# Layer norm of a four-layer transformer kernel: root applied on ScalarE, offset added by features behind the transposes

## The chip, the cores and the metric

One core of one Trainium2 chip runs the whole program. The metric is the device time of one execution in microseconds. Engines are called TensorE (PE in the profile; PEld is its weight load), VectorE (DVE), ScalarE (ACT), GpSimd (POOL), and SyncE (SP), which only issues transfers.

## What is computed

Four transformer layers over 256 tokens of 1024 features in f32: MLA attention, differential attention, a short convolution mixer and an mLSTM mixer, with six feed-forward blocks between and behind them (two with squared relu, four gated by silu). Behind each of the ten mixers and blocks stands the same layer norm over a residual:

```python
def _layernorm(x, g, b):
    mu = jnp.mean(xf, axis=-1, keepdims=True)
    var = jnp.mean(jnp.square(xf - mu), axis=-1, keepdims=True)
    y = (xf - mu) * lax.rsqrt(var + LN_EPS) * g + b

x = _layernorm(DEEPNORM_ALPHA * x + m, ln_mix_g[i], ln_mix_b[i])
```

## The kernel before

**Precision.** Every product is made of three: both operands are split into a high part in fp32r and a low part (the difference), and `product` adds high x high, high x low and low x high in PSUM.

**Weights.** All weights stream through six slots of 128x2048, in one order of units written out at build time. SyncE loads unit i when unit i - 6 has been used (`load`). ScalarE makes `whi` (`split_hi`, L288), VectorE `wlo` (`split_lo`, L293). Each engine has a `Splitter`; `split.to(i)` splits every unit up to number i at that place of its own program, so the order of splits among other work is fixed by hand. A transfer that has not landed holds ScalarE there.

**Stages.** `stages` is mla, 0, diff, 1, 2, conv, 3, 4, ml, 5 (numbers are the feed-forward blocks; 0 and 1 have squared relu). Stage n ends in layer norm n. Norm 9 is followed by the output's transfer only.

**The tail of a stage.** `tail_tensor` multiplies by the last three or four units (the tail), for tile t = 0 and then t = 1 of 128 tokens, and in each for column halves j = 0 and 1, into PSUM bank 2t + j. Before the last unit's product of (1,1) it transposes the normalised x of tile 0: `ln_turn(0,0)` and `ln_turn(0,1)`, four 128x128 transposes each (L449). `tail_vector` is VectorE's part, in this order: residual (0,0), (0,1), `ln_normal` of tile 0, residual (1,0), `ln_low` (0,0), (0,1), residual (1,1), `ln_normal` of tile 1, `ln_low` (1,0), (1,1). The residual is `res` = ALPHA x + bank (L500) and its statistics (L503). `ln_normal` aggregates, makes the root by a seed and three Newton steps on 128x1 columns (L508 to L520), then for each half centres and multiplies by the gain (L526) and multiplies by the root and adds the offset into x (L529). `tail_scalar` makes the high part of each transposed half out of PSUM, `ln_high`, one instruction of 128x512 (L484); `ln_low` is the matching difference (L488).

**The head of the next stage.** For norms 0, 2, 3, 4, 5, 6, 8, `head_tensor` multiplies the first two units with tokens as rows: tile 0's eight chunks of features, tile 1's eight. It needs `wait_x(t, half)`, the low part of that half. Before tile 0's last chunk stands `ln_turn(1,0)`, behind it `ln_turn(1,1)`, so TensorE waits there for x of tile 1. `head_scalar` copies the results (L646) and splits further units between. Norm 1 is followed by the q projection of diff (`diff_tensor`), norm 7 by the first products of ml, with the same transposes among them.

**gb** holds gain and offset of the current norm, broadcast over partitions; GpSimd reloads it (L540) when x of the norm is finished.

**Column parameters.** Some vectors are loaded at the start as rows of `res` by SyncE (`start_loads`, L2310), transposed on TensorE (`params_tensor`), and copied to `par`, where `col(name, c)` is a 128x1 column.

Of the kernel before, what the change touches and what calls it, by code (L numbers as in the profile page):

```python
# [19 lines left out]
F32 = mybir.dt.float32  # L20
# [6 lines left out]
P = 128  # L27
# [21 lines left out]
def build(nc, a, out):  # L49
# [29 lines left out]
    with ctx:  # L79
# [66 lines left out]
        rows.append(("q_norm", a["mla_q_norm"][0].rearrange("(c p) -> c p", p=P)))  # L146
        rows.append(("kv_norm", a["mla_kv_norm"][0].rearrange("(c p) -> c p", p=P)))
        rows.append(("subln", a["diff_subln"]))
        rows.append(("conv_w", a["conv_w_2"][0].rearrange("w (c p) -> (w c) p", p=P)))
        rows.append(("qk_conv_w", a["qk_conv_w_2"][0].rearrange("w (c p) -> (w c) p", p=P)))  # L150
        COL, row_dmas, at = {}, [], 0
# [191 lines left out]
        rope_ang = sem("rope_ang")  # L343
        rope_sin = sem("rope_sin")
        acc_bank = sem("acc_bank")
        ln_x = sem("ln_x")
        ln_t = sem("ln_t")
        x_hi = sem("x_hi")
# [109 lines left out]

        HC = KC // 2

        def turned(n, t, h):

            return 4 * (n + 1) + 2 * t + h + 1

        def turn_bank(n, t, h):
            return 6 + h if n >= 0 else 4 + 2 * t + h

        def turn_view(n, t, h):
            return ps[:, turn_bank(n, t, h), :].rearrange("p (c s) -> p c s", s=P)

        def half_x(tile, t, h):
            return tile[:, h * HC:(h + 1) * HC, t * P:(t + 1) * P]

        def ln_turn(pe, n, t, h):
            if n >= 0:
                pe.wait_ge(ln_x, 4 * n + 2 * t + h + 1)
            for c in range(HC):
                k = h * HC + c
                m = T(ps[:, turn_bank(n, t, h), c * P:(c + 1) * P], x[:, t, k * P:(k + 1) * P])
            m.then_inc(ln_t, 1)  # L480

        def ln_high(act, n, t, h):
            act.wait_ge(ln_t, turned(n, t, h))
            nc.scalar.activation(half_x(xthi, t, h), turn_view(n, t, h), ACT.Copy).then_inc(x_hi, 1)  # L484

        def ln_low(dve, n, t, h):
            dve.wait_ge(x_hi, turned(n, t, h))
            nc.vector.tensor_tensor(half_x(xtlo, t, h), turn_view(n, t, h),  # L488
                                    half_x(xthi, t, h).bitcast(F32), ALU.subtract).then_inc(x_lo, 1)

        def wait_x(pe, n, t, h):
            pe.wait_ge(x_lo, turned(n, t, h))

        def ln_residual(dve, link, n, t, j, last_unit):
            if 2 * t + j < 3:
# [9 lines left out]
        def ln_normal(dve, link, n, t):  # L505

            dve.wait_ge(link.s, link.n)
            link(nc.vector.bn_aggr(mv[:, t, :], stats[:, 2 * t:2 * t + 2, :].rearrange(  # L508
                "p a b -> p (a b)")))
            v, w, k = nt[:, 1, t:t + 1], nt[:, 1, TT + t:TT + t + 1], nt[:, 0, t:t + 1]  # L510
            y = rs[:, t:t + 1]
            link.mark(nc.vector.tensor_scalar_add(v, mv[:, t, 1:2], LN_EPS))
            link.mark(nc.vector.tensor_scalar(w, mv[:, t, 1:2], LN_EPS, -0.5, ALU.add, ALU.mult))
            dve.wait_ge(link.s, link.n - 1)
            link(nc.vector.tensor_scalar(y.bitcast(I32), v.bitcast(I32), -0.5, RSQRT_SEED,
                                         ALU.mult, ALU.add))
            for _ in range(3):
# [14 lines left out]

        def ln_gpsimd(pool, n):

            pool.wait_ge(ln_x, 4 * (n + 1))
            load_gb(pool, n + 1)

        def load_gb(pool, n):
# [35 lines left out]
        def tail_vector(dve, link, n, split, last_unit, upto):  # L574

            split.to(upto)
            ln_residual(dve, link, n, 0, 0, last_unit)
            ln_residual(dve, link, n, 0, 1, last_unit)
            ln_normal(dve, link, n, 0)
# [5 lines left out]
            ln_normal(dve, link, n, 1)  # L585
# [12 lines left out]
        def head_tensor(pe, n, head, banks, between):  # L598
# [9 lines left out]
            wait_split(pe, head[1])  # L608
            for t in range(TT):
                for c in range(KC):  # L610
                    if c % HC == 0:
                        wait_x(pe, n, t, c // HC)
# [102 lines left out]
        def ffn_scalar(act, f, split):  # L715
# [9 lines left out]
            for s in range(f.steps):  # L725
# [23 lines left out]
        def ffn_vector(dve, link, f, split):  # L749
            base, n = ffn_base[f.k], FFN_LN[f.k]  # L750

            def add(kind, s):
# [215 lines left out]
        def mla_tensor(pe):  # L968
# [11 lines left out]
            for group, bank0 in ((dq, 0), (dkv, 2)):  # L980
                for j, u in enumerate(group):
                    wait_split(pe, u)
                    for t in range(TT):
                        for c in range(4):
                            if c == 0 and bank0 == 0:
                                wait_x(pe, -1, t, j)
# [311 lines left out]
        def diff_tensor(pe):  # L1298
# [5 lines left out]
                                    j == 0, j == 3)  # L1304

            for t in range(TT):
                wait_x(pe, 1, t, 0)
                for j in range(2):
                    wait_split(pe, q[j])
                    project(q[j], j, 0, t, 0)  # L1310
                    if t == 0 and j == 1:
# [8 lines left out]
            for j in range(2, 4):  # L1320
                wait_split(pe, q[j])
                for t in range(TT):
                    wait_x(pe, 1, t, 1)
# [174 lines left out]

        def diff_vector(dve, link, split):
            q, k, v, o = (diff_u[4 * g:4 * g + 4] for g in range(4))  # L1500
            for n, group in enumerate((q, k)):
                for j, u in enumerate(group):
                    if n == 0 or j < 3:
# [202 lines left out]
        def conv_vector(dve, link, split):  # L1706
# [30 lines left out]
            def token(i):  # L1737
                wait_done(dve, conv_unit(i, 2))
                if i >= 2:
# [2 lines left out]
                                        c_s[:, i % 2].rearrange("p a b -> p (a b)"),  # L1742
                                        ps[:, c_bank(2), :], ALU.mult).then_inc(c_tok, 1)

            split.to(conv_u[5].index)
            taps(0)
            split.to(conv_u[6].index)
# [92 lines left out]
        def ml_tensor(pe):  # L1840
# [74 lines left out]
                                 stop=True, skip_group_check=True).then_inc(L["l_num"], 1)  # L1915

            for t in range(TT):
                wait_x(pe, 7, t, 0)
                for j in range(2):
                    wait_split(pe, VG[j])  # L1920
                    m = token_pieces(VG[j], j, t)
                    if t == 1:
# [4 lines left out]
            for j in range(2, 4):  # L1927
                wait_split(pe, VG[j])
                for t in range(TT):
                    wait_x(pe, 7, t, 1)  # L1930
# [166 lines left out]
        def ml_vector(dve, link, split):  # L2097
# [66 lines left out]
                                                 l_h[:, t, h * MD:(h + 1) * MD]))  # L2164

            link(nc.vector.memset(l_v[:, :, :, MD:], 1.0))
            for u in VG[:-1]:
                split.after(u)
            wait_done(dve, VG[-1])
# [154 lines left out]
        def params_tensor(pe):  # L2324

            pe.wait_ge(row_loaded, 16 * N_ROW_DMAS)
            wait_x(pe, -1, 1, 1)
# [179 lines left out]
```

## Time and profile before

| | us |
|---|---|
| median of 3 runs | 1588.84 (1588.3 to 1589.53) |
| the profiled execution | 1589.45 |
| its span in the profile | 1587.6 |
| TensorE busy | 1554.6 (98%) |
| VectorE busy | 1077.0 (68%) |
| ScalarE busy | 753.1 (47%) |
| granted TensorE clock, mean | 0.997 of full speed |

The profile is of one execution, and durations below come from it. Its span runs from the first instruction to the last; the profiled execution's own time is 1.85 us longer. Engines run side by side, so busy shares don't add up; a microsecond counts when the engine that sets the end stands still for it.

### The profile page before, as it was taken

The page shows a single profiled execution, that of the slowest core. Times are in us where ns is not written, and L with a number is a line of the kernel's source. Part 1 is how long each engine was busy: PE and PEld are TensorE (multiplying, and loading weights), DVE is VectorE, ACT ScalarE, POOL GpSimd, SP SyncE. Part 2 cuts the span into 40 slices and gives each one's busy share as a digit, 9 for nine tenths or more (in the row PEclk, how much of TensorE's full clock was granted, in tenths as well). Part 3 has the DMA queues.
Part 4 walks back from the last instruction along what each step waited for, and adds up shares of the span by engine and source line. Part 5 has one row for each costly group of instructions (what it writes and reads, how often), then busy time and mean ns, then how long its engine had stood idle before and what let it go on. Part 6 is the DMA issues. An engine that isn't in the chain of part 4 may idle for free.

```text
span 1587.6 us, 20708 instructions
## 1 busy us (share of the span) xinstructions
PE 1554.6 (98%) x8570; PEld 1337.1 (84%) x8570; DVE 1077.0 (68%) x1390; ACT 753.1 (47%) x874; POOL 18.5 (1%) x77
## 2 busy tenths in 40 slices
PE   7999999999999999999999999999999999999997
PEld 6978888799888888888888888887888798888886
DVE  6876666768766577655777665577555868965557
ACT  4735444457354443545454354444454365444542
POOL 1000000000000000000000000000000000000000
PEclk9999999999999999999999999999999999999999
DMA  8446565643565556555464655547555462365551
GB/s 265 134 160 212 188 193 176 212 160 114 171 209 197 186 186 209 188 186 187 165 206 133 212 186 189 194 149 239 185 186 188 157 209 95 132 239 185 186 191 48
DMA packets 198444, 285.97 MB, mean 180 GB/s; under 512 B 9287, under 2 KB 167055, under 8 KB 198351
## 3 DMA queue, kind: packets, MB, share of 16 engines
q1 hardware_dynamic: 194943, 272.20, 52.4%
q0 software_dynamic: 3264, 11.93, 2.3%
q8 instruction: 68, 1.11, 0.3%
q10 hardware_dynamic: 144, 0.52, 0.1%
q14 instruction: 25, 0.20, 0.0%
HBM read 283.58 MB, written 1.05 MB: 179 GB/s over the span
## 4 chain that ended last, share of the span: by engine, by line
PE 87%; DVE 9%; ACT 2%; issue 1%; DMA 1%; SPq 0%; DVEq 0%; ACTq 0%
PE ps L397 44%; PE ps L426 25%; PE ps L430 13%; PE ps L449 2%; DVE wlo L293 2%; DVE x L529 1%; DVE res L526 1%; ACT whi L288 1%; DVE stats L503 1%; DVE res L500 1%; DVE xt L488 1%; DMA raw<-in_mla_w_dq 1%; DVE nt L518 1%; PE ps L1574 1%; PE ps L1582 1%
## 5 line engine op out<-in xcount | busy, mean ns | idle before, releaser
L293 DVE TENSOR_TENSOR wlo<-raw,whi 128x2048 fp32r<-128x2048 f32 (+2 forms) x259 | 576.6, 2256 | 227.1 <-ACT whi L288 226.0
L288 ACT ACTIVATE whi<-raw 128x2048 fp32r<-128x2048 f32 (+2 forms) x262 | 483.1, 1879 | 19.6 <-DMA raw<-in_w_in_mlstm 4.7
L397 PE MATMUL ps<-whi,yt 128*128 128x512 f32 (+1 forms) x1472 | 460.9, 386 | 0.5 <-DVE wlo L293 0.5
L426 PE MATMUL ps<-xt,whi 128*128 128x512 f32 x1728 | 431.7, 392 | 0.0
L426 PEld LDWEIGHTS ps<-xt,whi 128*128 128x128 f32 x1728 | 314.2, 189 | 58.6
L397 PEld LDWEIGHTS ps<-whi,yt 128*128 128x128 f32 x1472 | 274.8, 188 | 54.8 <-DVE wlo L293 0.9
L397 PE MATMUL ps<-wlo,yt 128*128 128x512 f32 (+1 forms) x736 | 283.7, 386 | 0.0
L430 PEld LDWEIGHTS ps<-xt,wlo 128*128 128x128 f32 x1728 | 235.7, 190 | 16.9
L430 PE MATMUL ps<-xt,wlo 128*128 128x256 f32 x1728 | 240.9, 282 | 0.0
L397 PE MATMUL ps<-whi,xt 128*128 128x512 f32 (+4 forms) x778 | 222.4, 364 | 3.4 <-DVE wlo L293 2.5
L721 ACT ACTIVATE arena<-ps 128x512 f32<-128x512 f32 x108 | 64.1, 594 | 281.4 <-PE ps L430 281.4
L397 PEld LDWEIGHTS ps<-whi,xt 128*128 128x128 f32 x778 | 142.1, 192 | 27.7 <-DVE wlo L293 2.9
L754 DVE TENSOR_TENSOR arena<-arena,ps 128x512 f32<-128x512 f32 x108 | 73.9, 684 | 126.5 <-ACT arena L721 126.5
L397 PEld LDWEIGHTS ps<-wlo,yt 128*128 128x128 f32 x736 | 138.6, 188 | 24.7
L397 PE MATMUL ps<-wlo,xt 128*128 128x512 f32 (+4 forms) x389 | 139.5, 359 | 0.0
L484 ACT ACTIVATE xt<-ps 128x512 fp32r<-128x512 f32 x40 | 23.2, 596 | 187.7 <-PE ps L449 187.6
L744 ACT ACTIVATE yt<-arena 128x512 fp32r<-128x512 f32 x76 | 48.0, 632 | 124.8 <-DVE arena L774 69.5
L397 PE MATMUL ps<-xt,whi 128*128 128x256 f32 x560 | 102.7, 285 | 0.0
L397 PEld LDWEIGHTS ps<-xt,whi 128*128 128x128 f32 x560 | 87.1, 192 | 3.6 <-issue 3.6
L784 DVE TENSOR_TENSOR yt<-arena,yt 128x512 fp32r<-128x512 f32 x76 | 52.6, 693 | 53.1 <-ACT yt L744 53.1
L397 PEld LDWEIGHTS ps<-wlo,xt 128*128 128x128 f32 x389 | 75.0, 193 | 9.0
L397 PE MATMUL ps<-xt,wlo 128*128 128x256 f32 x280 | 79.2, 283 | 0.0
(229 smaller groups left out, 920.6 us busy)
## 6 DMA issues: line engine op xcount, KB each, us to landing
raw<-in_ffn_w_up SPq DMA_DIRECT2D x76, 1024.0 KB, 5.4
raw<-in_ffn_w_down SPq DMA_DIRECT2D x76, 1024.0 KB, 4.9
raw<-in_ffn_w_gate SPq DMA_DIRECT2D x44, 1024.0 KB, 5.3
raw<-in_diff_w_qkv SPq DMA_DIRECT2D x12, 1024.0 KB, 5.1
raw<-in_w_in_conv SPq DMA_DIRECT2D x10, 1024.0 KB, 5.4
raw<-in_w_out SPq DMA_DIRECT2D x8, 1024.0 KB, 4.9
raw<-in_w_in_mlstm SPq DMA_DIRECT2D x7, 1024.0 KB, 7.3
raw<-in_w_in_mlstm SPq DMA_DIRECT2D x8, 768.0 KB, 4.2
```

The lines of the kernel that those rows point to most:

```text
L288: nc.scalar.activation(whi[:, u.slot, 0:u.size], raw[:, u.slot, 0:u.size], ACT.Copy).then_inc(w_hi[u.slot], 1)
L293: nc.vector.tensor_tensor(wlo[:, u.slot, 0:u.size], raw[:, u.slot, 0:u.size], whi[:, u.slot, 0:u.size].bitcast(F32), ALU.subtract).then_in ...
L397: m = nc.tensor.matmul(out_, p, q, start=first and n == 0, stop=last and n == 2, skip_group_check=True)
L426: nc.tensor.matmul(o.rearrange("p (a n) -> p a n", a=2), parts[c][0], xt2[:, :, c, :], start=c == 0, stop=False, skip_group_check=True)
L430: m = nc.tensor.matmul(o[:, S:2 * S], parts[c][1], xthi[:, c, :], start=False, stop=c == KC - 1, skip_group_check=True)
L449: return nc.tensor.transpose(o, i, ident[0:i.shape[0], 0:i.shape[0]])
L484: nc.scalar.activation(half_x(xthi, t, h), turn_view(n, t, h), ACT.Copy).then_inc(x_hi, 1)
L488: nc.vector.tensor_tensor(half_x(xtlo, t, h), turn_view(n, t, h), half_x(xthi, t, h).bitcast(F32), ALU.subtract).then_inc(x_lo, 1)
L721: nc.scalar.activation(f_half(kind == "U" and f.gated), both_halves(f_bank(f, kind, s), 1), ACT.Copy).then_inc(f_part, 1)
L744: nc.scalar.activation(h_part(s, 0), f_view(1), ACT.Copy).then_inc(f_hi, 1)
L754: nc.vector.tensor_tensor(f_half(2 + (kind == "U" and f.gated)), f_half(kind == "U" and f.gated), both_halves(f_bank(f, kind, s), 0), ALU. ...
L784: nc.vector.tensor_tensor(h_part(s, 1), f_view(1), h_part(s, 0).bitcast(F32), ALU.subtract).then_inc(f_lo, 1)
```

## The change

Layer norms 0 to 8 are divided differently:

- VectorE's `ln_centre` (the old `ln_normal`) only centres and multiplies by the gain, both halves without a wait between. ScalarE's new `ln_scale` multiplies by the root (a column as scale), from `res` into x, 128x512.
- The transposes take x without the offset. `ln_high` and `ln_low` add it from a column of `par`, one chunk of 128 features at a time: four instructions of 128x128 each where one of 128x512 stood. Nine row loads of 8x128 bring the columns at the start; the rows then need two transposes and copies instead of one, and one of the old row blocks is cut in two.
- Tile 1 is turned in quarters of two chunks, each with its own PSUM bank (4 to 7) and its own signals; tile 0 stays in halves (banks 6 and 7). The waits of the next stage go by quarters for tile 1.
- The x that the next residual reads gets its offset later, by `ln_offset`, four additions of 128x512 on VectorE early in the next stage; the next tail and GpSimd's reload of gb wait for it.
- ScalarE splits one unit more between tile 0's highs and tile 1's scaling (before: behind the copy of the head's first result). In the gated blocks it splits the two head units before and right behind the copy of the last "U" product instead of behind the last hidden part.
- Norm 9 keeps both VectorE instructions.

```diff
@@ rows of parameters
+        for n_ in range(N_LN - 1):
+            rows.append((f"ln_b{n_}", layer_norm_params(n_)[1].rearrange("(c p) -> c p", p=P)))
@@ transposes
         def ln_turn(pe, n, t, h):
             if n >= 0:
                 pe.wait_ge(ln_x, 4 * n + 2 * t + h + 1)
-            for c in range(HC):
-                k = h * HC + c
-                m = T(ps[:, turn_bank(n, t, h), c * P:(c + 1) * P], x[:, t, k * P:(k + 1) * P])
-            m.then_inc(ln_t, 1)
+            for p in ln_pieces(n, t, h):
+                for c in piece_chunks(n, t, p):
+                    m = T(turn_view(n, t, p, c), x[:, t, c * P:(c + 1) * P])
+                m.then_inc(ln_t, 1)
+        def ln_scale(act, n, t, h):
+            act.wait_ge(ln_centred, 4 * n + 2 * t + h + 1)
+            half = slice(h * 512, h * 512 + 512)
+            nc.scalar.activation(x[:, t, half], res[:, t, half], ACT.Copy,
+                                 scale=rs[:, t:t + 1]).then_inc(ln_x, 1)
@@ ln_high, n >= 0
-            act.wait_ge(ln_t, turned(n, t, h))
-            nc.scalar.activation(half_x(xthi, t, h), turn_view(n, t, h), ACT.Copy).then_inc(x_hi, 1)
+            for p in ln_pieces(n, t, h):
+                act.wait_ge(ln_t, turned(n, t, p))
+                for c in piece_chunks(n, t, p):
+                    m = nc.scalar.activation(xthi[:, c, t * P:(t + 1) * P], turn_view(n, t, p, c),
+                                             ACT.Identity, bias=col(f"ln_b{n}", c))
+                m.then_inc(x_hi, 1)
@@ ln_low, n >= 0
+            for p in ln_pieces(n, t, h):
+                dve.wait_ge(x_hi, turned(n, t, p))
+                for c in piece_chunks(n, t, p):
+                    m = nc.vector.scalar_tensor_tensor(
+                        out=xtlo[:, c, t * P:(t + 1) * P], in0=turn_view(n, t, p, c),
+                        scalar=col(f"ln_b{n}", c), in1=xthi[:, c, t * P:(t + 1) * P].bitcast(F32),
+                        op0=ALU.add, op1=ALU.subtract)
+                m.then_inc(x_lo, 1)
@@ ln_normal, now ln_centre
-                link(nc.vector.scalar_tensor_tensor(
+                nc.vector.scalar_tensor_tensor(
                     out=res[:, t, half], in0=res[:, t, half], scalar=mv[:, t, 0:1],
-                    in1=gb[:, 0, half], op0=ALU.subtract, op1=ALU.mult))
-                nc.vector.scalar_tensor_tensor(
-                    out=x[:, t, half], in0=res[:, t, half], scalar=y, in1=gb[:, 1, half],
-                    op0=ALU.mult, op1=ALU.add).then_inc(ln_x, 1)
+                    in1=gb[:, 0, half], op0=ALU.subtract, op1=ALU.mult).then_inc(ln_centred, 1)
+        def ln_offset(dve, n):
+            for t in range(TT):
+                for h in range(2):
+                    half = slice(h * 512, h * 512 + 512)
+                    nc.vector.tensor_tensor(x[:, t, half], x[:, t, half], gb[:, 1, half],
+                                            ALU.add).then_inc(ln_done, 1)
@@ tail_scalar
-            for t in range(TT if n < N_LN - 1 else 0):
-                for h in range(2):
-                    ln_high(act, n, t, h)
+            ln_scale(act, n, 0, 0)
+            ln_scale(act, n, 0, 1)
+            ln_high(act, n, 0, 0)
+            ln_high(act, n, 0, 1)
+            split.to(upto + 1)
+            for h in range(2):
+                ln_scale(act, n, 1, h)
+                ln_high(act, n, 1, h)
@@ ffn_scalar
-                split.to(f.unit["U", s].index + (TAIL if f.gated and s >= f.steps - 2 else 2))
+                split.to(f.unit["U", s].index + (TAIL + (s == f.steps - 1)
+                                                 if f.gated and s >= f.steps - 2 else 2))
                 if f.gated and f.unit["U", s] not in f.head:
                     part("U", s)
+                    if s == f.steps - 1:
+                        split.to(f.tail[0].index + 4)
@@ ffn_vector (diff, conv and ml alike, behind their third or fourth unit)
+            split.to(f.head[1].index + 1)
+            ln_offset(dve, FFN_LN[f.k])
             split.to(f.head[1].index + 3)
@@ tail_vector
             split.to(upto)
+            dve.wait_ge(ln_done, 4 * n)
```

## Rows read from the trace of the kernel before

**Rows 1.** The page, part 1: busy us (share of the span) xinstructions.
```profile
PE 1554.6 (98%) x8570; PEld 1337.1 (84%) x8570; DVE 1077.0 (68%) x1390; ACT 753.1 (47%) x874; POOL 18.5 (1%) x77
```
**Rows 2.** Table of waits: who <- for whom: us in total, times, longest.
```profile
PEld ps L449 <- DVE x L529: 17.6, 24, 1.4
...
PE ps L449 <- DVE x L529: 8.2, 15, 1.0
```
**Rows 3.** Chain of waits at norm 0: start us, us, what.
```profile
104.11 0.61 ACT xt L484
...
104.74 1.29 DVE xt L488 x2
106.03 0.61 DVE res L500
...
109.36 0.76 DVE res L526
...
113.06 5.73 PE ps L397 x27
```
**Rows 4.** Timeline at norm 0, TensorE: start us, us, engine, line [idle before].
```profile
105.55 0.19 PEld L397 LDWEIGHTS ps<-whi,xt 128*128 128x128 f32 x1
...
110.95 0.66 PE L449 MATMUL ps<-ident,x 128*128 128x128 f32 x4 [0.28 <-DVE x L529]
...
111.37 0.47 PE L397 MATMUL ps<-whi,xt 128*128 128x512 f32 x1
```
**Rows 5.** Chain of waits at norm 1.
```profile
290.90 0.66 PE ps L449 x4
...
293.38 5.48 PE ps L397 x24
```
**Rows 6.** Timeline at norm 4, the engines together.
```profile
774.85 0.60 ACT L721 ACTIVATE arena<-ps 128x512 f32<-128x512 f32 x1 [2.03 <-PE ps L430]
...
779.47 4.50 DVE L293 TENSOR_TENSOR wlo<-raw,whi 128x2048 fp32r<-128x2048 f32 x2 [1.18 <-ACT whi L288]
...
788.61 0.75 DVE L526 SCALAR_TENSOR_TENSOR res<-res,mv,gb 128x512 f32<-128x512 f32 x1
...
790.20 0.66 PE L449 MATMUL ps<-ident,x 128*128 128x128 f32 x4 [0.40 <-DVE x L529]
...
791.65 0.66 PE L449 MATMUL ps<-ident,x 128*128 128x128 f32 x4 [0.79 <-DVE x L529]
...
794.02 0.68 DVE L500 SCALAR_TENSOR_TENSOR res<-x,ps 128x512 f32<-128x512 f32 x1
```
**Rows 7.** Chain of waits at norm 8.
```profile
1388.01 0.76 DVE res L526
...
1393.51 0.60 DVE res L500
```
**Rows 8.** Groups by line and shape: count | busy us, mean ns | idle before.
```profile
L737 ACT ACTIVATE arena<-arena 128x512 f32<-128x512 f32 x40 | 25.3, 632 | 44.6 <-DVE arena L754 44.6
...
L1464 ACT ACTIVATE xt<-ps,small 128x512 fp32r<-128x512 f32 x4 | 2.5, 707 | 0.0
...
L1555 DVE SCALAR_TENSOR_TENSOR xt<-ps,small,xt 128x512 fp32r<-128x512 f32 x4 | 2.7, 744 | 0.0
...
L1176 DVE SCALAR_TENSOR_TENSOR xt<-ps,par,xt 128x256 fp32r<-128x256 f32 x5 | 2.1, 477 | 0.0
```
**Rows 9.** Timelines of ScalarE and VectorE where small instructions follow one another.
```profile
62.70 0.37 ACT L913 ACTIVATE arena<-ps,small 128x128 f32<-128x128 f32 x1
62.96 0.19 ACT L913 ACTIVATION_READ_ACCUMULATOR arena<-ps,small 128x1 f32 x1
...
32.30 1.26 DVE L1176 SCALAR_TENSOR_TENSOR xt<-ps,par,xt 128x256 fp32r<-128x256 f32 x3
```
**Rows 10.** Timeline of the start: a row load, and the parameters' transpose.
```profile
10.57 0.32 SPq L2310 DMA_DIRECT2D res<-in_qk_conv_w  x1
...
21.84 0.23 PE L449 MATMUL ps<-ident,res 72*128 72x72 f32 x1
```

More of the change, by code:

```diff
@@ L345, in build @@
         acc_bank = sem("acc_bank")
+        ln_centred = sem("ln_centred")
+        ln_done = sem("ln_done")
         ln_x = sem("ln_x")
@@ L459, in build, with ln_chunks, ln_pieces, turned @@
         HC = KC // 2
[L461 to L469, printed above, removed]
+        def ln_chunks(n, t):
+            return HC // 2 if t == 1 and n >= 0 else HC
+        def ln_pieces(n, t, h):
+            k = HC // ln_chunks(n, t)
+            return range(h * k, (h + 1) * k)
+        def turned(n, t, p):
+            return 2 * t + p + 1 if n < 0 else 2 * TT + 6 * n + 2 * t + p + 1
+        def turn_bank(n, t, p):
+            if n < 0:
+                return 4 + 2 * t + p
+            return (4 if t else 6) + p
+        def piece_chunks(n, t, p):
+            return range(p * ln_chunks(n, t), (p + 1) * ln_chunks(n, t))
+        def turn_view(n, t, p, c):
+            k = c - piece_chunks(n, t, p)[0]
+            return ps[:, turn_bank(n, t, p), k * P:(k + 1) * P]
         def half_x(tile, t, h):
             return tile[:, h * HC:(h + 1) * HC, t * P:(t + 1) * P]
+        def half_turned(t, h):
+            return ps[:, turn_bank(-1, t, h), :].rearrange("p (c s) -> p c s", s=P)
         def ln_turn(pe, n, t, h):
@@ L476, in ln_turn @@
                 pe.wait_ge(ln_x, 4 * n + 2 * t + h + 1)
-            for c in range(HC):
-                k = h * HC + c
-                m = T(ps[:, turn_bank(n, t, h), c * P:(c + 1) * P], x[:, t, k * P:(k + 1) * P])
-            m.then_inc(ln_t, 1)
-        def ln_high(act, n, t, h):
-            act.wait_ge(ln_t, turned(n, t, h))
-            nc.scalar.activation(half_x(xthi, t, h), turn_view(n, t, h), ACT.Copy).then_inc(x_hi, 1)
-        def ln_low(dve, n, t, h):
-            dve.wait_ge(x_hi, turned(n, t, h))
-            nc.vector.tensor_tensor(half_x(xtlo, t, h), turn_view(n, t, h),
-                                    half_x(xthi, t, h).bitcast(F32), ALU.subtract).then_inc(x_lo, 1)
@@ L491, in wait_x @@
-        def wait_x(pe, n, t, h):
-            pe.wait_ge(x_lo, turned(n, t, h))
+            for p in ln_pieces(n, t, h):
[7 more added lines that the diff above has]
+                                 scale=rs[:, t:t + 1]).then_inc(ln_x, 1)
@@ new lines, in ln_high @@
+        def ln_high(act, n, t, h):
+            if n < 0:
+                act.wait_ge(ln_t, turned(n, t, h))
+                nc.scalar.activation(half_x(xthi, t, h), half_turned(t, h), ACT.Copy).then_inc(x_hi, 1)
+                return
+            for p in ln_pieces(n, t, h):
[4 more added lines that the diff above has]
+                m.then_inc(x_hi, 1)
@@ new lines, in ln_low @@
+        def ln_low(dve, n, t, h):
+            if n < 0:
+                dve.wait_ge(x_hi, turned(n, t, h))
+                nc.vector.tensor_tensor(half_x(xtlo, t, h), half_turned(t, h),
+                                        half_x(xthi, t, h).bitcast(F32),
+                                        ALU.subtract).then_inc(x_lo, 1)
+                return
+            for p in ln_pieces(n, t, h):
[6 more added lines that the diff above has]
+                m.then_inc(x_lo, 1)
@@ L494, in ln_residual, with wait_x @@
+        def wait_x(pe, n, t, c):
+            pe.wait_ge(x_lo, turned(n, t, c // ln_chunks(n, t)))
         def ln_residual(dve, link, n, t, j, last_unit):
@@ L503, in ln_residual, with ln_centre @@
             link.mark(nc.vector.bn_stats(stats[:, 2 * t + j, :], res[:, t, half]))
-        def ln_normal(dve, link, n, t):
+        def ln_centre(dve, link, n, t):
             dve.wait_ge(link.s, link.n)
@@ L525, in ln_normal @@
                 half = slice(h * 512, h * 512 + 512)
-                link(nc.vector.scalar_tensor_tensor(
+                nc.vector.scalar_tensor_tensor(
                     out=res[:, t, half], in0=res[:, t, half], scalar=mv[:, t, 0:1],
-                    in1=gb[:, 0, half], op0=ALU.subtract, op1=ALU.mult))
-                nc.vector.scalar_tensor_tensor(
-                    out=x[:, t, half], in0=res[:, t, half], scalar=y, in1=gb[:, 1, half],
-                    op0=ALU.mult, op1=ALU.add).then_inc(ln_x, 1)
+                    in1=gb[:, 0, half], op0=ALU.subtract, op1=ALU.mult).then_inc(ln_centred, 1)
+                if n == N_LN - 1:
+                    dve.wait_ge(ln_centred, 4 * n + 2 * t + h + 1)
+                    nc.vector.scalar_tensor_tensor(
+                        out=x[:, t, half], in0=res[:, t, half], scalar=y, in1=gb[:, 1, half],
+                        op0=ALU.mult, op1=ALU.add).then_inc(ln_x, 1)
+        def ln_offset(dve, n):
[4 more added lines that the diff above has]
+                                            ALU.add).then_inc(ln_done, 1)
         def ln_gpsimd(pool, n):
-            pool.wait_ge(ln_x, 4 * (n + 1))
+            pool.wait_ge(ln_done, 4 * (n + 1))
             load_gb(pool, n + 1)
@@ L576, in tail_vector @@
             split.to(upto)
+            dve.wait_ge(ln_done, 4 * n)
             ln_residual(dve, link, n, 0, 0, last_unit)
             ln_residual(dve, link, n, 0, 1, last_unit)
-            ln_normal(dve, link, n, 0)
+            ln_centre(dve, link, n, 0)
             ln_residual(dve, link, n, 1, 0, last_unit)
@@ L584, in tail_vector @@
             ln_residual(dve, link, n, 1, 1, last_unit)
-            ln_normal(dve, link, n, 1)
+            ln_centre(dve, link, n, 1)
             if n < N_LN - 1:
@@ L591, in tail_scalar @@
             split.to(upto)
-            for t in range(TT if n < N_LN - 1 else 0):
-                for h in range(2):
-                    ln_high(act, n, t, h)
+            if n == N_LN - 1:
+                return
+            ln_scale(act, n, 0, 0)
[6 more added lines that the diff above has]
+                ln_high(act, n, 1, h)
         HEAD_OF = {}
@@ L610, in head_tensor @@
                 for c in range(KC):
-                    if c % HC == 0:
-                        wait_x(pe, n, t, c // HC)
+                    if c % ln_chunks(n, t) == 0:
+                        wait_x(pe, n, t, c)
                     if (t, c) == (0, KC - 1):
@@ L985, in mla_tensor @@
                             if c == 0 and bank0 == 0:
-                                wait_x(pe, -1, t, j)
+                                wait_x(pe, -1, t, j * HC)
                             m = product(ps[:, bank0 + t, 0:u.dims[1]],
@@ L1306, in diff_tensor @@
             for t in range(TT):
-                wait_x(pe, 1, t, 0)
                 for j in range(2):
+                    wait_x(pe, 1, t, 2 * j)
                     wait_split(pe, q[j])
@@ L1322, in diff_tensor @@
                 for t in range(TT):
-                    wait_x(pe, 1, t, 1)
+                    wait_x(pe, 1, t, 2 * j)
                     for n in range(2):
@@ L1500, in diff_vector @@
             q, k, v, o = (diff_u[4 * g:4 * g + 4] for g in range(4))
+            split.to(q[3].index)
+            ln_offset(dve, 1)
             for n, group in enumerate((q, k)):
@@ L1743, in token @@
                                         ps[:, c_bank(2), :], ALU.mult).then_inc(c_tok, 1)
+            split.to(conv_u[2].index)
+            ln_offset(dve, 4)
             split.to(conv_u[5].index)
@@ L1917, in ml_tensor @@
             for t in range(TT):
-                wait_x(pe, 7, t, 0)
                 for j in range(2):
+                    wait_x(pe, 7, t, 2 * j)
                     wait_split(pe, VG[j])
@@ L1929, in ml_tensor @@
                 for t in range(TT):
-                    wait_x(pe, 7, t, 1)
+                    wait_x(pe, 7, t, 2 * j)
                     m = token_pieces(VG[j], j, t)
@@ L2166, in ml_vector @@
             link(nc.vector.memset(l_v[:, :, :, MD:], 1.0))
+            split.to(VG[3].index)
+            ln_offset(dve, 7)
             for u in VG[:-1]:
@@ L2326, in params_tensor @@
             pe.wait_ge(row_loaded, 16 * N_ROW_DMAS)
-            wait_x(pe, -1, 1, 1)
+            wait_x(pe, -1, 1, HC)
             for k in range(PAR_TILES):
```

## The prediction

> **What bounds the kernel now.** I read the page's busy shares first: TensorE is busy 98% of the span [rows 1], so this is a TensorE kernel, and an edit on another engine counts only where TensorE waits. The table of waits says where: the only repeated wait of TensorE is that of the transposes (L449) for the normalised tile x (L529), 17.6 and 8.2 us in the rows of its two halves, which overlap [rows 2]. So I read the chain of waits and the timeline around the layer norms, naming a norm n = 0 to 9, a transposed half T(t,h), and its two product operands high (ACT L484) and low (DVE L488).
>
> There are two kinds. In the **plain** kind (n = 0, 1, 2, 3, 5; the five show the same chain, n = 0 stands for them) the chain leaves TensorE after T(0,0), T(0,1), goes through high, both lows, and then the residual of (1,1), which was ready but queued behind the lows on VectorE: 104.11, 104.74, 106.03 [rows 3]. From there it is VectorE alone until x(1,1), and TensorE is back at 113.06. In the **late** kind (n = 4, 6, 7, 8) VectorE is behind already when the tail starts: splits of weights end at 783.97, TensorE then waits 0.40 and 0.79 us for x(0,0) and x(0,1), and residual (1,1) starts at 794.02 [rows 6]. In both, whatever delays the end of the low of (0,1) delays residual (1,1), the root, x(1,0), x(1,1) and the head's second tile, one for one. Norm 9 ends the program by the same two VectorE operations as before: nothing.
>
> **Prices of the new small instructions.** The change turns one instruction over 512 elements into four over 128 with a column as operand, for the high and for the low. No row shows just these.
> ScalarE, 128 wide out of PSUM with a column as bias: 0.37 us, the next instruction 0.26 us after its start [rows 9]. So four take 3 x 0.26 + 0.37 = 1.15 us against 0.61, eight 2.19.
> VectorE, 256 wide with a column, out of PSUM: 477 ns, three in 1.26 us, so a step of 0.39; 512 wide the duration is 744, so 128 elements fewer save 0.13: 0.26 a step, 0.34 alone [rows 8, 9]. Four take 1.12 us, eight 2.16, against 1.29 for the two big ones [rows 3].
> ScalarE's scaling over 512 out of SBUF with a column: 632 ns without a column [rows 8]; out of PSUM the column makes 707 out of about 600 [rows 8, 6]; so 0.74.
> Cheap end: the column costs nothing, 0.15 a step and 0.26 alone on ScalarE, 0.20 and 0.28 on VectorE (from 1.29 for two of 512), 0.63 for the scaling. Dear end: no overlap at all, 0.37 and 0.34 a step. The row of ScalarE has the very shape, and three of VectorE have the operand, so I take the middle values.
>
> **A plain norm, step by step.** With s = 104.11 (high begins):
> 1. High (0,0) is done at s + 1.15, low (0,0) starts at s + 1.18, both lows end at s + 1.18 + 2.16 = s + 3.34. Before: 106.03 = s + 1.92. So +1.42. (High (0,1) is done at s + 2.19, just ahead of its low.) TensorE waits too: its head starts at 105.55 [rows 4] and now needs low (0,0) at s + 2.33; this is hidden in the longer wait that follows, since T(1,0) depends on the VectorE chain.
> 2. Centre (1,0) to T(1,0): before 110.95 - 109.36 = 1.59 [rows 3, 4]. Now centre 0.76, hand-over 0.03, scaling 0.74, hand-over 0.04 = 1.57. Taking L529 off VectorE here buys 0.02: ScalarE is no faster at it. The second half is where it should pay, but see 3.
> 3. T(1,0) to the first product of the head's second tile: before 113.06 - 110.95 = 2.11. Now ScalarE does, in its queue, four highs of (1,0), then the scaling of (1,1): first quarter transposed 0.45, four steps of 0.26 = 1.04, scaling 0.74, hand-over 0.04, then T(1,1) 0.42 [rows 4] and 0.04 to the product: 2.73. So +0.62. The centred half (1,1) was ready 0.8 us before, but stands behind the highs; TensorE's T(1,1) is ahead of the second tile in its queue, so quartering doesn't let the product begin.
> Sum: 1.42 - 0.02 + 0.62 = 2.0 us. Four such norms: 8.0. Norm 1 had 293.38 - 290.90 = 2.48 for step 3 [rows 5], so 2.73 adds 0.25: 1.6.
>
> **A late norm.** ScalarE now splits the first head weight in its idle time before 774.85 (2.03 us) and the second right after, so VectorE, which waited 1.18 us for it, begins some 1.0 earlier [rows 6]; everything to x(0,1) comes earlier, and T(0,0) goes when TensorE is ready, 789.80, instead of 790.20. High begins 0.70 after T(0,0) (0.66 and 0.04) at 790.55, the lows end at +3.34 = 793.9, against 794.1. So -0.2, and with steps 2 and 3 -0.2 - 0.02 + 0.62 = +0.4. The 1.2 us that TensorE gains at T(0,0), T(0,1) are lost again: the head starts sooner and waits at T(1,0). Norms 4, 6, 7: +1.1. Norm 8 has no earlier split: T(0,0) at 1388.01 + 0.76 + 0.03 + 0.74 + 0.04 = 1389.58, lows end 1393.62 against 1393.51 [rows 7]: +0.1 and so +0.7.
>
> **What costs nothing, and by what cover.** The four additions of the offset (4 x 0.6 = 2.4 us of VectorE a norm) stand behind the split of the unit after the head, where VectorE next waits for ScalarE's copy of the head's second tile, which TensorE releases some 5.7 us after the head's second tile begins; without that cover 2.4 us at a norm. The split moved ahead of the scaling of tile 1 (1.9 us of ScalarE) lies between s + 2.2 and the scaling at s + 7.5 (lows end at 3.34, 3.33 of small VectorE work as from 106.03 to 109.36, centre 0.79), if its load has landed. GpSimd's reload of gain and offset starts some 5 us later, with a whole stage ahead of it.
> At the start SP issues ten more small row loads (nine offsets, and one row block now cut in two) of 0.32 us [rows 10], which puts every weight load behind them 3.3 us back; TensorE wants the rows at 21.84 [rows 10], 8 us after the last would be issued. I count 0.3 for one more transpose and copy; without the cover up to 3.
>
> **Sum.** 8.0 + 1.6 + 1.1 + 0.7 + 0.3 = 11.7 us on the profiled execution's own 1589.45 = 1601.2. The median stands 0.6 lower, so I forecast 1600.5.
>
> **The Trainium skill on this.** The row shows 0.37 us and a step of 0.26 [rows 9]. "ScalarE: Activation LUTs", section "What ACT_TABLE_LOAD costs", gives an ACTIVATE with a pointer operand about 280 ns plus 0.833 ns an element and lets neighbours overlap by about 93 ns. By that, a 128-wide one is an estimated 387 ns with a step of 294, which would put 0.12 and 0.14 us more on steps 1 and 3, about 2 us on the whole. Rule and row differ by 0.03 a step; I keep the row.
>
> **The rivals.**
> (a) The small instructions are cheap (columns free). Place: the lows of tile 0. Lows end at s + 0.74 + 1.68 = s + 2.42: step 1 is +0.5, step 2 -0.14, step 3 0.45 + 0.60 + 0.63 + 0.50 = 2.18, +0.07: +0.4 for a plain norm, 0 for norm 1; a late one ends its lows at 790.55 + 2.42 = 792.97, -1.1, in all -1.2; norm 8 -1.0. Sum 1.7 - 3.6 - 1.0 + 0.3 = -2.6: 1586.2, not slower. Between this and the forecast it turns at about a fifth of the way from this end, at steps of 0.17 and 0.21. Against it: the 128-wide row itself. For it: only that none of the shown ones follows its own kind without a wait.
> (b) No overlap between the small ones: eight lows 2.72, four highs 1.48: step 1 is +2.3, step 3 +1.1: 3.4 a plain norm, 3.0 norm 1, 1.7 to 2.0 a late one: 24 us, 1612.5. Against it: three of VectorE's 256-wide ones in 1.26.
> (c) A wait for a transfer takes the place of the late kind's gain: ScalarE now asks for the second head weight at 775.35, 6 us after its slot came free, with the last high of the hidden tile queued behind; a load that lands at 777 makes TensorE wait up to 0.8 in three tails; or the start slips by 3. 1603 to 1606.
> (d) The change does what its name says, and TensorE never waits again for x: the residual is then not held by the lows. That needs a shorter VectorE chain; [rows 3] show the lows ahead of it in the queue, which the change leaves there. Its best would take the 8.2 us that the matmul half of TensorE waits for x [rows 2]: 1580.6.
>
> **Chances.** Forecast 0.66; (a) and its neighbourhood 0.11; (b) 0.06; (c) 0.13; (d) 0.04. A measurement tells 0.2% (3.2 us) from nothing. The forecast's own range by half-way prices is 1596 to 1605. The range for 8 in 10 takes in (c) and half of what lies between the forecast and (a): 1592.5 to 1606. Faster: (d) and an edge of (a), 0.05. Same: most of (a), 0.09. Slower: 0.86.
>
> **What would show it.** Right: the small VectorE instructions step at 0.26; a plain norm's residual (1,1) starts 3.3 us after its first high, not 1.9; the scaling of (1,1) starts right behind the fourth high of (1,0); TensorE waits some 0.9 us at the head's start, again at T(1,0) and at T(1,1); the period from T(1,0) to the second tile is 2.7. Wrong: if these small instructions stream faster than their nearest rows, if the late norms gain at T(1,0), or if a transfer holds ScalarE ahead of a scaling.

## The result, and the profile after

The changed kernel takes 1604.37 us (median of 5, 1602.67 to 1607.68) against 1588.31 us of before (median of 5, 1588.12 to 1589.53): a ratio of 1.0099, 95% interval 1.0088 to 1.0111. It is slower by 16 us; the forecast was 1600.5, in a range of 1592.5 to 1606. The profiled execution took 1604.92 us with a span of 1603.1, so 15.5 more than before in both.

The page's busy shares, as [rows 1]:
```profile
PE 1555.4 (97%) x8571; PEld 1337.6 (83%) x8571; DVE 1087.6 (68%) x1499; ACT 797.0 (50%) x1018; POOL 18.5 (1%) x77
```
TensorE does the same work within 1 us. All 15 us are time in which it stands still or runs at the lower clock. The table of waits, as [rows 2] (who, for whom, us in total, times, longest):
```profile
DVE xt L534 <- ACT xt L520: 45.1, 27, 4.3
...
PEld ps L453 <- ACT x L508: 24.0, 20, 1.9
PE ps L453 <- ACT x L508: 16.4, 18, 1.6
...
PE ps L401 <- DVE xt L534: 5.7, 9, 0.7
```
The matmul half of TensorE waited 8.2 us for VectorE's x; it now waits 16.4 for ScalarE's, and another 5.7 for the low of (0,0) at the head's start, once at each of nine norms.

The new instructions by line and shape (count | busy us, mean ns | idle before), as [rows 8]:
```profile
L520 ACT ACTIVATE xt<-ps,par 128x128 fp32r<-128x128 f32 x144 | 40.2, 376 | 29.3 <-PE ps L453 29.1
L508 ACT ACTIVATE x<-res,rs 128x512 f32<-128x512 f32 x36 | 25.6, 727 | 117.6 <-DVE res L575 117.6
```
```profile
L534 DVE SCALAR_TENSOR_TENSOR xt<-ps,par,xt 128x128 fp32r<-128x128 f32 x144 | 39.7, 343 | 45.1 <-ACT xt L520 45.1
```
Norm 0 in the timeline, the engines together, as [rows 3, 4]:
```profile
104.22 2.18 ACT L520 ACTIVATE xt<-ps,par 128x128 fp32r<-128x128 f32 x8 [4.38 <-PE ps L453]
...
105.40 2.16 DVE L534 SCALAR_TENSOR_TENSOR xt<-ps,par,xt 128x128 fp32r<-128x128 f32 x8 [4.29 <-ACT xt L520]
...
106.68 0.47 PE L401 MATMUL ps<-whi,xt 128*128 128x512 f32 x1 [0.67 <-DVE xt L534]
...
107.48 0.67 DVE L549 SCALAR_TENSOR_TENSOR res<-x,ps 128x512 f32<-128x512 f32 x1
...
110.88 1.42 DVE L575 SCALAR_TENSOR_TENSOR res<-res,mv,gb 128x512 f32<-128x512 f32 x2
...
111.67 0.72 ACT L508 ACTIVATE x<-res,rs 128x512 f32<-128x512 f32 x1 [2.98 <-DVE res L575]
...
112.45 0.66 PE L453 MATMUL ps<-ident,x 128*128 128x128 f32 x4 [0.76 <-ACT x L508]
...
112.92 1.14 ACT L520 ACTIVATE xt<-ps,par 128x128 fp32r<-128x128 f32 x4 [0.53 <-PE ps L453]
...
113.94 0.73 ACT L508 ACTIVATE x<-res,rs 128x512 f32<-128x512 f32 x1
...
114.73 0.66 PE L453 MATMUL ps<-ident,x 128*128 128x128 f32 x4 [0.93 <-ACT x L508]
...
115.14 0.47 PE L401 MATMUL ps<-whi,xt 128*128 128x512 f32 x1
```
Read it from the top. Eight highs take 2.18 us, the lows start when the first four are done and end at 107.56, and residual (1,1), queued behind them, begins as the last of them ends: 107.48, where it was 106.03 in the chain before. TensorE stops three times: 0.67 for the low, 0.76 for x(1,0), 0.93 for x(1,1). The scaling of (1,1) starts at 113.94, right behind four highs of (1,0), though its input was there at 112.30 (110.88 and 1.42).

Where the 15.5 us are, from TensorE's transposes of each norm in both timelines (the shift of one point against the same point before; a late norm is credited with the waits that go ahead of its own transposes, and the extra fall of the clock has a row of its own):

| place | forecast | measured |
|---|---|---|
| start, up to T(0,0) of norm 0 | 0.3 | 0.1 |
| norms 0, 2, 3, 5 | 2.0 each | 2.0 each |
| norm 1 | 1.6 | 1.9 |
| norms 4, 6 | 0.4 each | about 0.1 each |
| norm 7 | 0.4 | 1.5 |
| norm 8 | 0.7 | 0.7 |
| ml, between norms 7 and 8 | 0 | 1.5 |
| granted clock, behind norm 3 | 0 | 1.6 |

The last two rows are new mechanisms. In ml VectorE waits for a transfer:
```profile
1280.60 0.66 PE L453 MATMUL ps<-ident,x 128*128 128x128 f32 x4 [1.38 <-ACT x L508]
...
1282.88 1.12 PE L453 MATMUL ps<-ident,x 128*128 128x128 f32 x4 [1.62 <-ACT x L508]
...
1291.66 0.53 POOL L599 DMA_DIRECT2D gb<-in_ln_g  x1 [188.83 <-DVE x L589]
...
1293.24 0.54 POOL L2521 DMA_DIRECT2D g_bias<-in_b_gates  x1
...
1300.91 0.17 DVE L2250 TENSOR_TENSOR small<-ps,g_bias 128x16 f32<-128x16 f32 x1 [2.93 <-DMA g_bias<-in_b_gates]
```
Before, GpSimd issued this load 1.8 us after T(1,1) of norm 7, which was at 1269.42:
```profile
1271.23 0.54 POOL L2443 DMA_DIRECT2D g_bias<-in_b_gates  x1
```
Now it stands behind GpSimd's wait for the late offset (L589) and goes 10.4 us after T(1,1).

The clock: busy time by engine (PE, PEld, DVE, ACT, POOL), then the granted clock, DMA share, GB/s, in the changed kernel:
```profile
612.00:620.00 8.00, 6.37 (x28) 4.74 (x28) 6.37 (x23) 4.00 (x8) 0.00 (x0) 1.00 0.84 299
620.00:624.00 4.00, 3.48 (x11) 2.89 (x12) 2.72 (x7) 2.10 (x6) 0.00 (x0) 0.59 0.00 0
```
Behind norm 3's pauses TensorE runs near its lower level, 1.2 of 2.4 GHz, until about 624.

### The profile page after: what moved, and what is told of

It is laid out like the page before. It is cut to its first block and busy times, and to the rows that moved or that the text cites. A ratio compares the mean times of both kernels' runs of the same rounds, so it can differ in the third digit from the quotient of the medians.

```text
span 1603.1 us, 20987 instructions
## 1 busy us (share of the span) xinstructions
PE 1555.4 (97%) x8571; PEld 1337.6 (83%) x8571; DVE 1087.6 (68%) x1499; ACT 797.0 (50%) x1018; POOL 18.5 (1%) x77
## 5 line engine op out<-in xcount | busy, mean ns | idle before, releaser
L508 ACT ACTIVATE x<-res,rs 128x512 f32<-128x512 f32 x36 | 25.6, 727 | 117.6 <-DVE res L575 117.6
```

Source lines behind the costliest of these rows:

```text
L508: nc.scalar.activation(x[:, t, half], res[:, t, half], ACT.Copy, scale=rs[:, t:t + 1]).then_inc(ln_x, 1)
```

## Experiments

All were run in turns with the kernel before; medians, and the ratio to before with its 95% interval. The kernel before had medians of 1589.20 us beside e1 to e4, 1588.66 beside e5 to e8 and 1589.16 beside e9 and e10, and 1588.31 beside the changed kernel, so a difference between runs of two such groups is uncertain by up to 1 us from that alone.

**e1: tile 0 in wide instructions.** It leaves the offset out of tile 0's transposed x.
```diff
 ln_high, and ln_low alike, n >= 0
+            if t == 0:
+                act.wait_ge(ln_t, turned(n, t, h))
+                nc.scalar.activation(half_x(xthi, t, h), wide_view(t, h), ACT.Copy).then_inc(x_hi, 1)
+                return
```


> The changed kernel with tile 0's high and low parts made by one instruction of 128x512 each again; it leaves the offset out of tile 0's transposed x. Theory (the eight small VectorE and ScalarE instructions hold residual (1,1) back): the lows of tile 0 end 1.4 us sooner at every one of norms 0 to 8, TensorE no longer waits some 0.67 us at the head's start, and nine times 1.4 is 12.6 us: about 1591.8 against 1604.4 of the changed kernel. Rival (the hand-over of the scaling to ScalarE is what costs): the time stays within 2 us of 1604. A fall of TensorE's granted clock at one norm more or less moves either by 1.6.

Measured 1591.67 us (1.0017, 1.0008 to 1.0027): 12.7 less than the changed kernel. The head starts without a wait, T(1,0) is at 110.90 as in the kernel before (110.95), T(1,1) is still late:
```profile
110.90 0.66 PE L453 MATMUL ps<-ident,x 128*128 128x128 f32 x4 [0.25 <-ACT x L508]
...
113.18 0.66 PE L453 MATMUL ps<-ident,x 128*128 128x128 f32 x4 [0.93 <-ACT x L508]
```
So four fifths of the loss hang on eight small highs and eight small lows a norm. ScalarE still applies the root here, so the hand-over is not the cost of that part. That 12.7 is so near the forecast 12.6 is in part luck: in the profile norms 0 to 6 give 1.4 each as forecast and norm 8 1.3, the stretch from norm 7 to norm 8 gives only 0.6, and the clock falls once between the norms instead of twice, which is worth 1.6.

**e2: both tiles wide, both in halves.** It leaves the offset out of all transposed x.
```diff
 as e1 for both tiles, and
-            return HC // 2 if t == 1 and n >= 0 else HC
+            return HC
-            return (4 if t else 6) + p
+            return 6 + p
```


> As the one before, and tile 1 too is turned in halves with one high and one low of 128x512; it leaves the offset out of all transposed x. Theory: ScalarE's queue between T(1,0) and the scaling of (1,1) shortens from 0.45 + 1.04 to 0.70 + 0.49, so 0.3 us less at each norm than the run before: about 1589. Rival (quartering lets the second tile start early, so it is worth something): slower than the run before by 0.2 us a norm.

1587.69 us (0.9994, 0.9984 to 1.0003): 4.0 less than e1, no different from before. T(1,0) to T(1,1) is 1.95 us instead of 2.28. With the small instructions gone the change is neutral as a whole, and that is a sum of two parts: in its profile a plain norm still costs 0.2 to 0.25 more than before (norms 0, 1 and 2), and the splits of e5 give 2.5 back.

**e3: ScalarE's order for tile 1.**
```diff
-            for h in range(2):
-                ln_scale(act, n, 1, h)
-                ln_high(act, n, 1, h)
+            ln_scale(act, n, 1, 0)
+            ln_scale(act, n, 1, 1)
+            ln_high(act, n, 1, 0)
+            ln_high(act, n, 1, 1)
```


> The changed kernel with ScalarE's order for tile 1 as scale, scale, high, high. Theory (the scaling of (1,1) stands behind four highs): T(1,1) comes 1.35 us after T(1,0), when TensorE is ready, instead of 2.28; the head's second tile then waits for the first quarter's low at 1.9 behind T(1,0), against 2.69: 0.8 us less at seven head norms, 0.4 at norms 1 and 7: 6.4 us, about 1598. Rival (the highs and lows of (1,0) are what the second tile waits for): no difference.

1595.68 us (1.0043, 1.0028 to 1.0058): 8.7 less, 6.4 forecast. T(1,1) no longer waits; it comes 1.19 behind T(1,0):
```profile
112.67 0.66 PE L453 MATMUL ps<-ident,x 128*128 128x128 f32 x4 [0.74 <-ACT x L508]
...
113.86 0.60 PE L453 MATMUL ps<-ident,x 128*128 128x128 f32 x4
```
From T(0,0) to T(1,1) norm 0 took 11.15 us and takes 10.05; 0.24 of that comes back behind T(1,1), where the weight load waits 0.27 for the first low. In its profile the clock falls once (at 1276) where it fell twice in the changed kernel's, and a fall is worth 1.6. The profiles differ by 9.4 us: 1.6 of clock, 0.8 at each of seven head norms and 0.5 at norm 1 about as forecast, and 1.8 instead of 0.4 between the transposes of norms 7 and 8. So the forecast was short by the clock and by norm 7.

**e4: gate loads ahead of GpSimd's wait.**
```diff
+                if n == 7:
+                    pool.wait_ge(ln_x, 4 * (n + 1))
+                    (the two loads of l_gain and g_bias, moved up from behind)
                 ln_gpsimd(pool, n)
```


> The changed kernel with GpSimd issuing the two loads of ml's gain and gate offset when x of norm 7 is scaled, ahead of its wait for the late offset. Theory: VectorE's wait of 2.93 us for the gate offset goes, and with it the 1.56 us that TensorE loses between norm 7 and norm 8: 1602.8. Rival (the loss in ml comes from the four additions standing among VectorE's splits there): 1604.4, with the waits of TensorE for VectorE's convolution still in the trace.

1601.94 us (1.0082, 1.0065 to 1.0099): 2.4 less, 1.6 forecast. VectorE's addition no longer waits:
```profile
1283.70 0.54 POOL L2520 DMA_DIRECT2D g_bias<-in_b_gates  x1
...
1297.69 0.17 DVE L2250 TENSOR_TENSOR small<-ps,g_bias 128x16 f32<-128x16 f32 x1
```
T(1,1) of norm 7 to T(0,0) of norm 8 is 118.5 us against 121.6: 1.5 for the wait, and 1.6 because the clock did not fall behind norm 7 in this execution. It fell behind norm 6 instead. The pauses at norm 7 were the changed kernel's own (0.58, 1.39 and 1.63 us against 0.58, 1.38 and 1.62), so the loads are not shown to be what kept the clock there, though it did not fall behind norm 7 in the profiles of e7 and e8 either, which have them early too. Behind norm 3 the same stretch, with the same pauses and busy time as in the changed kernel, kept its clock:
```profile
612.00:620.00 8.00, 6.38 (x28) 4.74 (x28) 6.36 (x23) 4.00 (x8) 0.00 (x0) 1.00 0.82 293
620.00:624.00 4.00, 3.48 (x18) 2.95 (x19) 2.85 (x7) 2.10 (x6) 0.00 (x0) 1.00 0.00 0
```

**e5: the splits of the gated blocks alone, in the kernel before.**
```diff
+                split.to(f.unit["U", s].index + (TAIL + (s == f.steps - 1)
+                                                 if f.gated and s >= f.steps - 2 else 2))
 and behind part("U", s):
+                    if s == f.steps - 1:
+                        split.to(f.tail[0].index + 4)
```


> The kernel before with one edit of the change alone: in the last step of the gated blocks ScalarE splits the two head units before and right behind the copy of the last U product. Theory: VectorE reaches the tail's first residual 1.0 us sooner at norms 4, 6 and 7, TensorE waits less for x(0,0) and x(0,1), and the lows of tile 0 end about 1.0 us sooner: 3 us less in all, 1586.2. Rival (the load of the second head unit lands late and holds the last hidden part's high): no gain, or up to 2 us slower.

1586.15 us (0.9985, 0.9976 to 0.9994), as forecast. At norm 4 T(0,0) goes without a wait, T(0,1) waits 0.32 instead of 0.79:
```profile
788.78 0.60 PE L449 MATMUL ps<-ident,x 128*128 128x128 f32 x4
...
789.71 0.66 PE L449 MATMUL ps<-ident,x 128*128 128x128 f32 x4 [0.32 <-DVE x L529]
```
By the transposes in the two profiles it gives 1.1 at norm 4, 1.1 at norm 6 and 0.5 at norm 7. This part of the change is a gain by itself; rival (c)'s late load did not show.

**e6: tile 0 in small instructions, in the kernel before.** The column is one of zeros.
```diff
 ln_high, and ln_low alike
+            if n >= 0 and t == 0:
+                for c in range(HC):
+                    m = nc.scalar.activation(xthi[:, h * HC + c, 0:P], turn_view(n, t, h)[:, c, :],
+                                             ACT.Identity, bias=masks[:, 1, 0:1])
+                m.then_inc(x_hi, 1)
+                return
```


> The kernel before with tile 0's high and low alone made of four instructions of 128x128 with a column operand (a column of zeros, so the result is unchanged); VectorE still applies root and offset. Theory (the narrow instructions are the loss, wherever the root is applied): the lows end 1.4 us later at the five plain norms and 0.9 later at the four late ones: 10.7 us more, about 1600. Rival (narrow ones cost only together with ScalarE's scaling ahead of them in its queue): within 2 us of before.

1599.6 us (1.0069, 1.0055 to 1.0083): 10.9 more than before, 10.7 forecast. T(1,0) of norm 0 waits 0.77 as in the changed kernel, and nothing of the change but these instructions is in it:
```profile
112.41 0.66 PE L449 MATMUL ps<-ident,x 128*128 128x128 f32 x4 [0.77 <-DVE x L543]
...
113.86 0.66 PE L449 MATMUL ps<-ident,x 128*128 128x128 f32 x4
```

**e7: the change for tile 1 only.** Tile 0 as before, tile 1 as in e3, gate loads as in e4, late offset for tile 1.
```diff
-                if n == N_LN - 1:
+                if n == N_LN - 1 or t == 0:
 tile 0 wide as in e1; ln_offset for t = 1 only; no ln_scale for tile 0
```


> The changed kernel with tile 0 done as before (VectorE applies root and offset, one high and one low of 128x512), tile 1 by the change but with ScalarE's order scale, scale, high, high, the late offset for tile 1 only, and the gate loads early. Theory: the sum of what the three single edits gave (12.7 for tile 0, 8.7 for the order, 2.4 for the loads), less about 1 us at each of the four late norms for VectorE's scaling of tile 0: 1604.4 - 23.8 + 4 = 1584.6, faster than before by 0.3%. Rival (the gains are the same microseconds counted twice): 1588 or more.

1583.31 us (0.9968, 0.9956 to 0.9980), computing all of the reference, the fastest of all. At norm 0 T(0,0) to T(1,1) is 8.64 us against 8.93 before:
```profile
111.45 0.66 PE L453 MATMUL ps<-ident,x 128*128 128x128 f32 x4 [0.24 <-ACT x L508]
...
112.64 0.60 PE L453 MATMUL ps<-ident,x 128*128 128x128 f32 x4
```
With the scaling of (1,1) ahead of them, the small instructions of tile 1 do little harm that can be seen: TensorE's weight load waits 0.27 us for the first low behind T(1,1) of norm 0, 2.7 us in eight waits over the program (before, 1.9 in nine), and the norm is still shorter than before. No run has this order with wide instructions in tile 1, so what they cost here is not measured; in the changed kernel's order e1 against e2 puts them at 4.0 us, with quarters in e1 and halves in e2. Some 2.5 of its 5.3 us are the splits of e5; its profile shows no fall of the clock between norms 0 and 9, that of before one.

**e8: both repairs of order, tile 0 still small.** The edits of e3 and e4 together.

> The changed kernel with both repairs of order, the scaling first and the gate loads early, and tile 0 still in small instructions. Theory: 1595.7 less 1.6 to 2.4 for the loads: about 1593.7, still slower than before, since the small instructions of tile 0 remain. Rival (most of what the scaling first gave was TensorE's clock not falling, and it is the same clock that the loads' wait touches): 1595 or more.

1593.03 us (1.0030, 1.0018 to 1.0042), as forecast: order alone does not win back the loss.

**e9: tile 1 in halves, still small.**
```diff
-            return HC // 2 if t == 1 and n >= 0 else HC
+            return HC
-            return (4 if t else 6) + p
+            return 6 + p
```


> The changed kernel with tile 1 turned, signalled and awaited in halves as tile 0 (banks 6 and 7), its high and low parts still four small instructions a half. Theory: ScalarE's first high of (1,0) starts 0.21 us later (four transposes instead of two before it), so the scaling of (1,1) and T(1,1) do too: 0.2 us at seven to nine norms, about 2 us slower than the changed kernel: 1606. Rival (quartering gives nothing, since T(1,1) stands ahead of the second tile in TensorE's queue and the highs run on without a gap): within 0.5 us.

1608.69 us (1.0124, 1.0109 to 1.0139): 4.3 more, 2 forecast. T(1,0) to T(1,1) is 2.49 instead of 2.28, which is the forecast 0.2 a norm:
```profile
114.68 0.66 PE L453 MATMUL ps<-ident,x 128*128 128x128 f32 x4 [1.15 <-ACT x L508]
```
The rest is behind T(1,1): the first product of the second tile starts 0.55 us after it, where it was 0.41 (115.14 - 114.73).
```profile
115.23 0.50 PE L401 MATMUL ps<-whi,xt 128*128 128x512 f32 x1
```
From T(1,1) to T(0,0) of the next norm, norms 0 to 6 take 0.14 to 0.19 more than in the changed kernel, so the quarters were worth some 0.4 a norm, not 0.2, and the rival is out. The clock falls twice between the norms in both profiles (here at 1285 and 1418) and does not make the difference.

**e10: the late additions cut to one column.** The residual's x lacks the offset nearly everywhere.
```diff
-                    half = slice(h * 512, h * 512 + 512)
+                    half = slice(h * 512, h * 512 + 1)
```


> The changed kernel with the late additions of the offset cut to one column each (the residual's x then lacks the offset nearly everywhere), all their signals kept. Theory: seven of the nine places are covered by VectorE's wait for the next split, so little moves there; in ml the gate loads start 2 us sooner behind the shorter additions, which gives back some 1.5 us: about 1602.5. Rival (the additions delay splits everywhere): 2.4 us at each of nine norms, 1583.

1602.45 us (1.0089, 1.0072 to 1.0106): 1.9 less, as forecast. From norm 1 to norm 2 T(0,0) comes 141.9 us later in both, and at norm 7 it stands at 1270.16 against 1271.74, which is the one fall of the clock behind norm 3; so the additions cost nothing up to there. What it gains is in ml, 120.2 us from T(1,1) of norm 7 to T(0,0) of norm 8 against 121.6, each with one fall of the clock: GpSimd's wait ends sooner.

## Why the prediction was right, and where it was off

**Prices.** They held: 0.376 for a small high, a step of 0.25 (four in 1.14); 0.343 for a small low, a step of 0.26 (eight in 2.16); 0.727 for the scaling (0.74 assumed). "ScalarE: Activation LUTs" of the Trainium skill (section "What ACT_TABLE_LOAD costs") gives an estimated 387 and a step of 294; the trace's step is 0.04 us below it, so trace and page do not agree there, and the row of before was the better source. Rivals (a) and (b) are out by these rows.

**Step 1, the lows of tile 0.** Forecast +1.42; the lows end 3.34 us after the first high (107.56 against 104.22), where the step had put them. Of the 1.42, 0.55 are the first four highs (the first low starts 1.18 behind the first high, not 0.63) and 0.87 the eight lows (2.16 against 1.29); no run changed one of the two alone. The wait at the head's start was 0.67 us where 0.9 was named. That the later lows are the loss, and not the hand-over to ScalarE, e1 and e6 show from both sides: 12.7 less without the small instructions of tile 0, 10.9 more with nothing else.

**Step 2, the scaling.** Forecast 1.57 from centre to T(1,0); measured 112.45 - 110.88 = 1.57.

**Step 3, T(1,0) to the second tile.** Forecast +0.62; measured 2.69 against 2.11 by the chain's row of before (+0.58) or 2.07 by its timeline (+0.62). e3 shows that it is ScalarE's order.

**Norm 1.** It measured 0.3 more than the forecast 1.6; why is open.

**The late norms.** For 4 and 6 the forecast +0.4 was 0.3 too much, the sum of a few tenths. For norm 7 the step "Norms 4, 6, 7: +1.1" failed: it took norm 7 for norm 4. The head units behind norm 7 are 1552 wide, so VectorE's splits ended 1.4 us earlier in its tail than at norm 4 (1252.89 in a tail that began at 1245.03, against 783.97 in one that began at 774.65), and T(0,0) and T(0,1) went as one row of eight already:
```profile
1249.43 3.46 DVE L293 TENSOR_TENSOR wlo<-raw,whi 128x1552 fp32r<-128x1552 f32 x2 [0.77 <-ACT whi L288]
...
1260.02 1.22 PE L449 MATMUL ps<-ident,x 128*128 128x128 f32 x8
```
The early splits had only some 0.5 us to take there (e5), where they take 1.1 at norms 4 and 6. It measured +1.5: a plain norm's 2.0 less that 0.5.

**"A whole stage ahead of it".** The working let GpSimd's wait move from x to the late offset and named only the reload of gb behind it. Two more loads stand behind it in GpSimd's queue at norm 7, and VectorE wants one of them 15 us after T(1,1) (at 1297.98, which is 1300.91 - 2.93). That missed term is 1.5 us; e4 gives it back, and e10 most of it.

**The clock.** The working had no term for it. In the profile of before the granted clock falls once between the norms' start and the end of the last stage (1270 to 1273), in the changed kernel's twice (620 to 624, 1282 to 1286), and each of these falls costs 1.6 us: behind norm 3 TensorE needs 13.2 us from T(1,1) to the head's transposes, behind norm 2 and 5 11.6.

**The additions of the offset** were hidden as forecast, and the start's row loads too as far as can be told: the shift at T(0,0) of norm 0 is 0.1, but executions differ there by more than that (the kernel of e5, with no row load added, stands 0.9 earlier than before). Rival (c), a late load of weights, did not appear. Rival (d) needed a shorter VectorE chain, and VectorE's was longer.

So the way was right, and 3.8 us of the 15.5 in the profile were not in the forecast: 1.1 at norm 7, 1.5 in ml, 1.6 of clock, against 0.4 elsewhere.

## What to carry to other kernels

Before an instruction is cut in four, ask what is queued behind it on its engine: the same small instructions cost 11 us in tile 0, where the next residual stood behind them, some 4 us in tile 1 with the scaling of (1,1) behind them, and little that a trace shows in tile 1 with that scaling ahead. When work moves to a second engine, put it in that engine's queue ahead of what only waits for its turn: two lines exchanged gave back 8.7 us, part of it by the clock. When a wait is moved to a later signal, list every instruction behind it on that engine, transfers included, and the time at which each is wanted.

## What the hardware showed that was not expected

TensorE's clock fell from 2.4 to 1.2 GHz behind two or three pauses of 0.4 to 1.6 us each around a norm's transposes, and not at the same norm each time. With the same pauses of 0.67, 0.75 and 0.93 us it fell behind norm 3 in one execution and kept 2.4 GHz there in another, which fell behind norm 6; with 0.58, 1.4 and 1.6 at norm 7 it fell in the changed kernel and in e10 and not in e4. "TensorE: Matmul & The Clock Gate" of the Trainium skill (Part 1, "What you observe") has the point at which the clock rises at a kernel's start vary from run to run. The traces agree: the first record of 2.4 GHz is at 20.9 us in the trace of before, at 20.0 in the changed kernel's and at 11.8 in e1's. A plausible consequence, argued and not shown, is the wider spread of the changed kernel's times (5.0 us over 5 runs, 1.4 before): each fall is worth 1.6 us, and nine norms offer a chance of one. Its slowest run, of 1607.68 us, has the lowest mean granted clock, 0.994 against 0.996 to 0.997 in the others.
